# Another order of gathered rows and table tiles in the expert stage of a two-block layer kernel

## The reference

```python
def block(xt):                                   # 128 tokens
    q = (xt @ w_q).reshape(128, 8, 2, 128)
    sc = einsum('thcd,chnd->thcn', q, sub_keys)  # two sets of 128 scores
    ...                                          # best 16 of the 16 x 16 pairs -> idx, best_s
    g = softmax(best_s)
    pre = einsum('td,thkd->thk', xt, u[idx])
    coef = g * gelu(pre)
    return einsum('thk,thkd->td', coef, v[idx])
```

## Time and profile before

| | |
|---|---|
| median of 3 runs | 2452.94 us (2448.78 to 2458.18) |
| the profiled execution | 2435.17 us, its span 2433.4 us |
| PE busy | 2059.8 us, 85% |
| DVE busy | 1416.8 us, 58% |
| ACT busy | 549.4 us, 23% |
| GpSimd busy | 940.6 us, 39% |
| moved | 614.89 MB, mean 253 GB/s |
| mean granted TensorE clock | 0.877 |

### The profile page before, as it was taken

How to read it: one execution, slowest core, us unless ns; L and a number is a source line. 1 busy time by engine, 2 the same in 40 slices (tenths; PEclk the granted TensorE clock), 3 DMA queues, 4 the chain that set the end, 5 groups by cost and what they waited for, 6 DMA issues and landing times.

```text
span 2433.4 us, 22741 instructions
## 1 busy us (share of the span) xinstructions
PE 2059.8 (85%) x7874; PEld 1331.3 (55%) x7874; DVE 1416.8 (58%) x3213; ACT 549.4 (23%) x1524; POOL 940.6 (39%) x814
## 2 busy tenths in 40 slices
PE   6999999877699988877788799998898888886546
PEld 6777666566566664656576794443574333332212
DVE  0111134355878865789866779755557656445555
ACT  1111024312011111224321572000571111010111
POOL 2000000000335553657541503434373655566776
PEclk9999998789797888976898558999999999998779
DMA  5221333256676787988785706978687999999999
GB/s 155 104 104 69 121 143 138 78 208 216 207 277 210 251 318 267 383 301 286 271 302 208 293 4 209 351 292 330 220 273 258 370 349 365 339 362 390 357 385 345
DMA packets 190626, 614.89 MB, mean 253 GB/s; under 512 B 18096, under 2 KB 18096, under 8 KB 190512
## 3 DMA queue, kind: packets, MB, share of 16 engines
q0 software_dynamic: 111168, 403.64, 46.0%
q1 hardware_dynamic: 76400, 202.92, 22.5%
q10 hardware_dynamic: 2944, 6.89, 0.8%
HBM read 610.22 MB, written 3.15 MB: 252 GB/s over the span
## 4 chain that ended last, share of the span: by engine, by line
PE 60%; DVE 10%; POOL 9%; issue 9%; DMA 9%; ACT 2%; another core or an unknown queue 2%; ACTq 0%; SPq 0%; DVEq 0%; POOLq 0%
PE ps L1659 59%; POOL sb_arena L631 7%; DVE sb_arena L1147 3%; DMA sb_arena<-in_peer_u,sb_idx 2%; POOL sb_wring L631 2%; DMA sb_arena<-in_peer_v 2%; DMA sb_wring<-in_peer_v 1%; DMA sb_wring<-in_w_out 1%; DMA sb_gains<-in_norm_g 1%; DMA sb_wring<-in_peer_u,sb_idx 1%; DMA sb_wring<-in_peer_v,sb_idx 1%; DVE sb_arena L1599 1%; DMA sb_arena<-in_peer_v,sb_idx 1%; DMA sb_wring<-in_w_in 0%
## 5 line engine op out<-in xcount | busy, mean ns | idle before, releaser
L631 POOL DMA_INDIRECT sb_arena<-in_peer_u,sb_idx x405 | 523.1, 1292 | 1153.1 <-DVE sb_idx L1137 617.9
L1659 PE MATMUL ps<-sb_arena 128*128 128x64 f32 (+9 forms) x2576 | 654.0, 414 | 93.7 <-DMA sb_arena<-in_peer_v 39.7
L1659 PEld LDWEIGHTS ps<-sb_arena 128*128 128x128 f32 (+4 forms) x2576 | 437.5, 223 | 301.5 <-issue 211.3
L1659 PE MATMUL ps<-sb_arena,sb_wring 128*128 128x256 f32 (+2 forms) x2816 | 540.7, 354 | 45.7 <-issue 37.9
L1147 DVE CUSTOM_DVE_ANT_0 sb_arena<-sb_arena 128x1024 f32<-128x1024 f32 x405 | 480.8, 1221 | 105.9 <-DMA sb_arena<-in_peer_u,sb_idx 102.1
L1659 PEld LDWEIGHTS ps<-sb_arena,sb_wring 128*128 128x128 f32 x2816 | 473.2, 203 | 101.1 <-issue 44.4
L1659 PE MATMUL ps<-sb_wring,sb_arena 128*128 128x512 f32 (+3 forms) x1072 | 467.1, 594 | 53.3 <-DMA sb_wring<-in_peer_v 21.8
L1659 PEld LDWEIGHTS ps<-sb_wring,sb_arena 128*128 128x128 f32 (+1 forms) x1072 | 207.5, 196 | 301.4 <-issue 231.8
L631 POOL DMA_INDIRECT sb_arena<-in_peer_v,sb_idx x166 | 177.1, 1067 | 139.1 <-DVE sb_coef L1147 73.5
L1659 PE MATMUL ps<-sb_arena,sb_poolw 128*128 128x512 f32 (+1 forms) x388 | 181.8, 605 | 34.4 <-DMA sb_arena<-in_peer_v,sb_idx 28.3
L631 POOL DMA_INDIRECT sb_wring<-in_peer_u,sb_idx x107 | 132.2, 1235 | 113.6 <-PE ps L1659 89.5
(11 more groups left out here) (239 smaller groups left out, 1352.7 us busy)
## 6 DMA issues: line engine op xcount, KB each, us to landing
sb_wring<-in_w_in SPq DMA_DIRECT2D x52, 1024.0 KB, 7.4
sb_arena<-in_peer_v SPq DMA_DIRECT2D x70, 512.0 KB, 12.2
sb_wring<-in_peer_w_q SPq DMA_DIRECT2D x32, 1024.0 KB, 7.4
sb_wring<-in_peer_v SPq DMA_DIRECT2D x58, 512.0 KB, 11.7
sb_wring<-in_w_o SPq DMA_DIRECT2D x16, 1024.0 KB, 7.0
sb_wring<-in_w_out SPq DMA_DIRECT2D x8, 1024.0 KB
sb_arena<-in_peer_u,sb_idx POOLq DMA_INDIRECT x405
sb_arena<-in_x ACTq DMA_DIRECT2D x8, 512.0 KB, 8.0
```

The source lines that it names most:

```text
L631: nc.gpsimd.indirect_dma_start(gathered[buf(n)], None, table, bass.IndirectOffsetOnAxis(ap=idx[:, t, at_:at_ + 1], axis=0))\
L1659: return nc.tensor.matmul(o, l, r, start=start, stop=stop)
```

## The change

The order list is another one, and the start of the stage is arranged for it.

- Ahead of the tiles stand the u rows of three heads (16, 17, 18) instead of two.
- The first 64 tiles are cut into eights, each followed by a u head (19 to 26); before, into twelves, followed by u heads 18 to 22.
- With the second build stand the dots of u27 and u28 (32 rows, one for each step) and the order of gathers u27, v16, u28, v17; before, the dots of u23 and the order u23, v16, v17.
- The second 64 tiles have u29, u30 and the v heads 18 to 25 among them: u29, 12 tiles, v18; u30, 12 tiles, v19; then v20, 12 tiles, v21 and so on to v25; four tiles. Before: u24 to u28 each ahead of 12 tiles and v18 to v22 behind them; v23, u29, four tiles.
- After the last tile come v26, v27, u31, v28 to v31 (112 rows). Before: v24 to v26, u30, v27, v28, u31, v29 to v31 (160 rows).
- The first 22 places of the stage use the ten `KEYS` buffers, then the first four `early` ones, then the eight of `RING`. So that `dense_w` may be written over the early ones, 14 dots of head 16 and `tops_of(18)` stand ahead of the first build's picks; the rest of head 16, head 17, `tops_of(19)` and 7 rows of head 18 are taken one at a time after its steps.
- `rank` and `rank_u` move from the first early buffer to the place of `pick_a`.

```diff
--- before.py
+++ after.py
@@ -1,4 +1,5 @@
 from contextlib import ExitStack
+from itertools import chain
 
 import numpy as np
 
@@ -198,8 +199,8 @@
         pick_a = cut(after, 2, PICK, HALF)
         rank_t = cut(after + 2 * PICK * HALF, 3 * TG, P)
         pick_j = [cut(skT_at + n * PICK * P, PICK, P) for n in range(2)]
-        rank = cut(layer_end, 2, TG * H * TOPK)
-        rank_u = cut(layer_end + 2 * TG * H * TOPK, 2, TG * H * TOPK).bitcast(U32)
+        rank = cut(after, 2, TG * H * TOPK)
+        rank_u = cut(after + 2 * TG * H * TOPK, 2, TG * H * TOPK).bitcast(U32)
         x2r = cut(tb, TG, D)
         ostage = cut(tb + TG * D, D)
 
@@ -465,19 +466,21 @@
 
         CHUNKS = NT * H
         EARLY = [("u", k) for k in range(EARLY_CHUNKS)]
-        SEQ = [("u", 16), ("u", 17)]
+        SEQ = [("u", 16), ("u", 17), ("u", 18)]
         tiles = iter(range(NK))
 
         def stream(n):
             return [("d", next(tiles)) for _ in range(n)]
 
-        for m in range(18, 23):
-            SEQ += stream(12) + [("u", m)]
-        SEQ += stream(4) + [("b", 0), ("u", 23), ("v", 16), ("v", 17)]
-        for m in range(24, 29):
-            SEQ += [("u", m)] + stream(12) + [("v", m - 6)]
-        SEQ += [("v", 23), ("u", 29)] + stream(4) + [("v", k) for k in range(24, 27)]
-        SEQ += [("u", 30), ("v", 27), ("v", 28), ("u", 31), ("v", 29), ("v", 30), ("v", 31)]
+        for m in range(19, 27):
+            SEQ += stream(8) + [("u", m)]
+        SEQ += [("b", 0), ("u", 27), ("v", 16), ("u", 28), ("v", 17)]
+        for m in (29, 30):
+            SEQ += [("u", m)] + stream(12) + [("v", m - 11)]
+        for k in range(20, 26, 2):
+            SEQ += [("v", k)] + stream(12) + [("v", k + 1)]
+        SEQ += stream(4) + [("v", 26), ("v", 27), ("u", 31)] + [("v", k) for k in range(28, CHUNKS)]
+        WITH_FIRST, WITH_SECOND = (16, 17, 18), (27, 28)
         WITH_BUILD = (16, 17)
         order_of_dmas, place = [], {}
         for kind, k in EARLY + SEQ:
@@ -499,14 +502,18 @@
                 v_at[k, j] = taken[on_vector(k, j)]
                 taken[on_vector(k, j)] += 1
 
+
+        opening = list(KEYS) + list(range(4)) + list(RING)
         first_ring = list(KEYS) + list(RING)
         second_ring = list(OVER) + list(SCORES) + first_ring
 
         def buf(n):
             if n < LATE:
                 return n % EARLY_BUFS
+            if n < LATE + len(opening):
+                return opening[n - LATE]
             if n < OPEN:
-                return first_ring[(n - LATE) % len(first_ring)]
+                return first_ring[(n - LATE - len(opening)) % len(first_ring)]
             return second_ring[(n - OPEN) % len(second_ring)]
 
         uses, count_of, had, seen = {}, {}, {}, {}
@@ -1208,35 +1215,34 @@
                 yield from tops_of(2 * H, 2 * H + 1)
                 while not dense_over[0]:
                     yield
-                k_top, k_w = 2 * H + 3, 2 * H
+                k_top, k_w = 2 * H + 4, 2 * H
+                first_rows = dots(16)
+                for _ in range(len(KEYS) + 4):
+                    next(first_rows)
+                yield from tops_of(18)
+                third_rows = dots(18)
+                between = chain(first_rows, dots(17), tops_of(19), third_rows)
+                for b in range(BUILDS):
+                    picks(b)
+                    next(between)
+                for _ in between:
+                    pass
                 for kind, k in SEQ:
                     if kind == "u":
-                        if k == 17:
-                            rows_, head = dots(k), tops_of(k + 1)
-                            for b in range(BUILDS):
-                                picks(b)
-                                if b < TOPK:
-                                    next(rows_)
-                                elif b % 2:
-                                    next(head, None)
-                            for _ in head:
-                                pass
-                        elif k != 23:
-                            if k > 17:
-                                for _ in range(3):
-                                    if k_top < CHUNKS and k_top < k + 5:
-                                        yield from tops_of(k_top)
-                                        k_top += 1
+                        if k not in WITH_FIRST + WITH_SECOND:
+                            for _ in range(3):
+                                if k_top < CHUNKS and k_top < k + 5:
+                                    yield from tops_of(k_top)
+                                    k_top += 1
                             yield from dots(k)
                         while k_w <= (CHUNKS - 1 if k == CHUNKS - 1 else k - LAG):
                             weigh(k_w)
                             k_w += 1
                     elif kind == "b":
-                        rows_ = dots(23)
+                        between = chain(*[dots(k_) for k_ in WITH_SECOND])
                         for b in range(BUILDS):
                             picks(BUILDS + b)
-                            if b < TOPK:
-                                next(rows_)
+                            next(between)
                     elif kind == "v" and k not in WITH_BUILD:
                         added(k)
                         if k in (26, 27, 28):
```

## The result

The changed kernel takes **2461.56 us** in the median (12 runs, 2454.3 to 2474.45); the kernel before, run beside it, 2448.88 (12 runs, 2442.73 to 2458.18). The ratio is **1.0054**, with a 95% interval of 1.0033 to 1.0076. The forecast was 2436 us, a ratio of 0.993. So some 13 us were lost where 17 were to be won. The new profiled execution took 2454.3 us, its span 2452.5: 19.1 more than the span before.

The account below looks back on a forecast made before the run. The bound moves: PE in the builds, a ring of 18 buffers in the tile stages, transfers in the tail. Terms -11.5 + 24.5 + 16.5 + 21.3 + 1 - 3 - 66 = -17.2 gave 2436 us, range 2406 to 2467.

Parts of the forecast that it names:

- Part 1: Start of first build: early buffers let 14 dots finish sooner, first tile at 1457.0 instead of 1468.5, -11.5 us.
- 2 first 64 tiles: First tile stage: groups of 8 tiles and 16 rows take 33.5 us each, +24.5 us, bounds +13 and +35.
- 3 hole: Before the second build's v rows: v16 queues behind u27 rows, hole 26.5 instead of 9.9 us, +16.5.
- 4 second build: Second build: v17 queues behind u28 on POOL, +19.5 us wait and +1.8 for the lower clock after it.
- Part 5: Restart of tiles after the second build: one block of tops less, but weigh(26) waits for ACT; 17 us, +1.
- Part 6: Second 64 tiles: four waits removed, about -38; v24, v25 added, +27.5; late last v rows, +8; together -3 us.
- Part 7: Tail: 48 fewer rows at 1.38 us, -66; v30's need of v28 and DVE's later wait called even.
- Rival (a): First build's clock: after the shorter pause PE keeps 2.4 GHz, stage 16 us shorter, 2420 us; chance 1 in 10.
- (b): Hole and second build: smaller because u28's rows are issued in time, -20, so 2416 us; chance 15 in 100.
- (c): First tiles: ring period 36.2 us, waited tile as slow as the median tile, +11 to +19, 2451; chance 2 in 10.
- (d): First tiles: waited tile's landing reaches 14 us, period 38, first half some 30 us more, 2466; chance 17 in 100.
- The step from the span to the median: Whole kernel: the timed median exceeds the profiled span by 17.8 us as before, taking 2416.2 to 2436 us.

Follow-up runs that it names:

- changed (D): The changed kernel without further edits, run on chip D of five chips A to E, against the kernel before beside it: 1.0013 (0.9987 to 1.0039).
- before, Gelu early (A): The kernel before with head 31's Gelu ahead of v29's diagonals instead of behind them, on chip A: 1.0013 of the kernel before.
- start alone: Kernel before with three heads' u rows ahead of the tiles, its order of the rest one head further on, chip B: 0.9888, 2423.17 us.
- rows in turn: Changed kernel with gathers of u27 and v16, then u28 and v17, alternating row by row: 0.9800 of the kernel before on chip A.
- Spreading the rows: Version with both pairs of the second build in turn, plus six tiles ahead of each of v20 to v25, chip E: 0.9771 of the kernel before.
- the variant on B: Apparently the kernel before with the rows of u23 and v16 gathered in turn: 0.9984 (0.995 to 1.0017) of the kernel before.
- the test with four gathers in flight: At most four gathers in flight behind the last tile, chip D, against the kernel before: changed kernel 1.0196, version in turn 0.9994.
- one head: Changed kernel with only u27 with the second build, u28 ahead of the first twelve tiles behind it, chip B: 0.9887 of the kernel before, 2424.43 us.

## Why the prediction was wrong

Against the trace of before, the forecast had -17.2 us and the trace of after has +19.1. By its parts:

| part | forecast | changed | changed (D) against before, Gelu early (A) |
|---|---|---|---|
| 1 start (first tile) | -11.5 | -6.0 | -13.3 |
| 2 first 64 tiles | +24.5 | +26.6 | +22.7 |
| 3 hole | +16.5 | +18.9 | +19.6 |
| 4 second build | +21.3 | +22.9 | +28.3 |
| 5, 6 restart, second tiles | -2 | +10.2 | +13.7 |
| 7 tail | -66 | -53.4 | -73.8 |

**Part 1 was right.** The pause before the build fell from 16.81 to 4.64 us and the stage kept its 109.46 us, so from the last product ahead of it the start is 12.1 shorter (126.9 to 114.8). The 6 us that the sum lacks are the dense part, which ended at 1347.7 instead of 1341.6; in the kernels that share its code it ended anywhere from 1342.6 to 1366.1. That is the span of one execution, no cost of the change. What the forecast overlooked is that the third head's rows are nearly free there (start alone, 0.9888): the start won more than I had given it.

**Rival (a) fell:** the granted clock was 0.50 all through the first build with the shorter pause as well.

**Parts 2 to 4 were right in mechanism and nearly in size.** The period of the first tiles was 37 to 40 us at first (group starts at 1524.83, 1564.58, 1601.88) and then 32.5 to 33.5, with a wait for a tile in each. v16's first row came 28.7 us after the last tile (forecast 26.5), and PE waited 20.89 us for v17 (forecast 19.5). Rivals (b), (c) and (d) did not come. The rows in turn show that 3 and 4 are one cost, the 16 u rows queued ahead of each 16 v rows: both left with it.

**Part 6 is a term that was mis-sized, by a mechanism I had named.** For 32 adjacent v rows I took 2.7 us a group above PE's 27.5, 8 us in all. The three groups took 32.1, 34.4 and 32.5 us from their first row to the next tile, 16.5 above PE's time, and 33.1, 33.9 and 34.1 on chip D, 18.6 above it. So 8.4 us of the miss come from there, and 10.5 on D. Spreading the rows won the whole of it back: in its trace six groups of eight rows take 13.7 to 14.0 each, and the second stage is 17.5 us shorter (373.4 to 355.9).

**Part 5** in the first trace: 22.9 us from the build to d66 instead of 17, and 19.2 on chip D. `weigh(26)` waited as foretold. d66 takes the buffer of u29's first row, so it waits for the block of tops and one dot on DVE and then for its own landing. On D the block took 8.9 us, as forecast, and d66 started 6.8 us after the dot instead of some 3, with DMA full (a share of 1.02 from 1906 to 1913 us), which I hadn't charged. In the first trace the landing was shorter (4.2), but the block took 15.2 us, since DVE waited for signals of its own instructions just before:

```profile
1905.52 0.17 DVE L1124 TENSOR_TENSOR sb_soft<-sb_arena 128x16 f32<-128x16 f32 x1 [2.12 <-remote]
...
1909.72 0.18 DVE L1128 CAST sb_arena<-sb_arena 128x32 f32<-128x32 uint32 x1 [3.83 <-remote]
```

That is the late signal again, on another engine. On B and C the changed kernel's d66 came 23.6 and 23.1 us after the build.

**Part 7 was wrong in kind.** I called it even that v30 needs rows of v28 and that DVE waits for the Gelu. By itself that was right: on chip D the wait is there, no gather stands, and the tail of 160.4 us is even shorter than the 171 of the forecast. But it is even only while ACT's diagonals keep pace. With the late signals, which the trace of before had as well, the v28 and v29 diagonals hold the Gelu back by some 20 us more, and the tail is 183.0, 178.5 and 184.4. In the kernel before the same stall lay in front of a longer wait, and its traces show little of it (a tail of 236.4 with, 234.2 without; the variant on B, with the stall, had 254.6, in an execution 18.3 us above its own median). Its own rows, which I had not followed up:

```profile
2246.95 0.40 ACT L996 ACTIVATE sb_poolw<-sb_ident,sb_coef 128x128 f32<-128x128 f32 x1 [11.49 <-remote]
2257.45 0.40 ACT L996 ACTIVATE sb_poolw<-sb_ident,sb_coef 128x128 f32<-128x128 f32 x1 [10.10 <-remote]
```

**The step from the span to the median** hid part of the miss. The span was forecast at 2416.2 and came out at 2452.5, 36.3 us longer; the median was forecast at 2436 and came out at 2461.56, 25.6 longer. I had added 17.8 us, and the profiled execution of after lay only 7.3 under its median. That the two errors had opposite signs is luck.

**The whole.** The forecast's balance was a sum of +62 and -80. Of the 36.3 us that the first trace's span lies above it, 12.6 are the tail, 12.2 the restart and the second tiles, 5.5 the dense part ahead of the stage, and 6 the other three parts. On chip D, where no signal is late, the miss is 14.4: 15.7 in the restart and the second tiles and 7.0 in the second build, less 7.8 in the tail. So the steps that failed are the "+8" for the last v rows of a group in part 6, and the word "even" in part 7, and the balance changed its sign. The hole and the wait of parts 3 and 4 cost most (42 us), but the forecast had them. What is settled: the changed kernel loses by the second head of u rows with the build, ahead of the v rows in one queue; by the adjacent v rows; and, where signals are late, by a longer restart and tail. How much of the ratio the late signals make isn't settled: the traces say some 20 us in the tail and 4 in the restart, the ratios without them and with them (1.0013 against 1.0016, 1.0054 and 1.0057) at most 11, and the kernel before is slower there too.

## What to carry to other kernels

Where two kinds of transfers share one queue and are used by different engines step by step, queue them in turn, row by row: two waits of 21 us were gone after an edit of the order. When moved work is charged with what it costs at its new place, look also at whether the place has room: the third head ahead of the tiles was nearly free. The second head with the build was not, until its rows were queued in turn with the v rows (0.9800 for two heads in turn, 0.9837 for one, 1.0013 to 1.0057 for two in blocks). And a wait that is called even should be priced once with the engine behind it late. Where an engine starts late though its inputs are in place, compare its start with the end of the instruction that frees its buffer, and not only with the inputs.

## What the runs showed of the hardware

On some chips the signals between engines came late while the gathers were at their full rate. Two to eight diagonals of a trace, in the tail or just ahead of it, started 6.5 to 40 us after PE had ended the row that frees their buffer, and 5 to 12 us after the instruction before them on ACT; the releaser is "remote" or "issue", and for most of them the trace records an increment of `v_used` 0.02 to 0.08 us ahead of the start. That was so in all twelve traces on B, C, E and wherever the first two were taken (before, changed, start alone, one head, in turn, spread), and in none of the eight on A and D. DVE's waits inside a block of tops, for its own instruction just before, split the same way: up to 3.83 us in nine of the twelve traces, and none above 0.4 us in the eight. The gathers moved about 410 GB/s in such stretches (2230 to 2275 us of before, 2353 to 2377 of changed) and as much without late signals (2250 to 2320 us of the version in turn on A, 2300 to 2370 of changed on D). So full transfers alone don't bring it, and it goes with the chip; the kernel before is also 14 to 24 us faster in the median on A and D. Why the increments are late was not shown: the test with four gathers in flight ran on a chip without it. It stays open. More than four buffers for diagonals might hide a part of it; no run tried that.

The first build's products of 64 columns kept PE busy for 109.46 us at a granted clock of 0.50 in both kernels, while the second build, with products of 512 columns between the same products, ran at 0.98 to 0.99 where it had no waits.
